# The first nine projection blocks on raw x, with the norm factor put on the results

## The reference

```python
def rmsnorm(x, g):
    x32 = x.astype(jnp.float32)
    r = lax.rsqrt(jnp.mean(x32 * x32, axis=-1, keepdims=True) + EPS)
    return (x32 * r * g.astype(jnp.float32)).astype(x.dtype)

def project_in(x, pos, g_attn_norm, w_in, ...):
    xn = rmsnorm(x, g_attn_norm)
    z = jnp.einsum('bsd,de->bse', xn, w_in)
    qa, ka, va, oa, ia, fa, cq, ckv, kr, gate_a, gate_b = split_cols(z)
    ...
```

## Time and profile before

| | us |
|---|---|
| median of the runs shown (three, 2769.88 to 2774.63) | 2773.61 |
| the profiled execution | 2768.64 |
| its span | 2766.5 |
| TensorE busy | 2729.1 |
| VectorE busy | 1638.6 |
| ScalarE busy | 1281.1 |
| GpSimd busy | 411.4 |

### The profile page before, as it was taken

The page is one execution under the profiler, slowest core; times in us unless marked ns, Lnnn a source line. Parts: engine busy times, 40 slices in busy tenths (PEclk is TensorE's granted clock), DMA queues, the critical chain, the costliest instruction groups (busy, mean ns, idle before and its releaser), DMA issues.

```text
span 2766.5 us, 54080 instructions
## 1 busy us (share of the span) xinstructions
PE 2729.1 (99%) x19156; PEld 2603.4 (94%) x19156; DVE 1638.6 (59%) x2739; ACT 1281.1 (46%) x2286; POOL 411.4 (15%) x770
## 2 busy tenths in 40 slices
PE   9998899999999999999999999999999999999999
PEld 9865799999999989999999999999999999999999
DVE  5466866666566654555454444466767644667754
ACT  5536665565556544444443333344444433444432
POOL 0102343443334310000000000022000000000010
PEclk9999999999999999999999999999999999999999
DMA  7524121221122177656657566576555456555575
GB/s 241 199 70 111 35 51 51 66 57 53 50 63 64 38 236 208 191 172 187 189 172 203 166 174 169 166 189 173 166 167 166 138 166 185 168 167 159 146 188 132
DMA packets 737356, 393.55 MB, mean 142 GB/s; under 512 B 109262, under 2 KB 719288, under 8 KB 736560
## 3 DMA queue, kind: packets, MB, share of 16 engines
q1 hardware_dynamic: 709132, 378.61, 47.7%
q10 hardware_dynamic: 27508, 11.54, 1.5%
q0 software_dynamic: 512, 0.83, 0.3%
HBM read 370.49 MB, written 22.75 MB: 142 GB/s over the span
## 4 chain that ended last, share of the span: by engine, by line
PE 60%; DVE 1%; issue 1%; ACT 1%; ACTq 0%; DVEq 0%
PE bank L302 19%; PE bank L307 19%; PE bank L303 19%; PE bank L2748 0%; ACT sqm L2812 0%; PE bank L2726 0%; PE bank L2736 0%; DVE hn L2913 0%; PE bank L2733 0%; PE bank L2722 0%; DVE hn L2908 0%; ACT dws L2806 0%; DVE ns L2895 0%; PE bank L2721 0%; PE bank L2710 0%
## 5 line engine op out<-in xcount | busy, mean ns | idle before, releaser
L290 DVE TENSOR_TENSOR w_lo_b<-stage,w_hi_b 128x2048 fp32r<-128x2048 f32 (+2 forms) x286 | 612.4, 2142 | 404.6 <-ACT w_hi_b L283 400.1
L283 ACT ACTIVATE w_hi_b<-stage 128x2048 fp32r<-128x2048 f32 (+1 forms) x284 | 508.3, 1790 | 559.4 <-PE bank L307 496.0
L302 PE MATMUL bank<-xnH,w_hi_b 128*128 128x288 f32 (+1 forms) x2736 | 741.0, 299 | 2.6 <-PEq L191 2.6
L303 PE MATMUL bank<-xnL,w_hi_b 128*128 128x288 f32 (+1 forms) x2736 | 735.6, 295 | 0.0
L302 PEld LDWEIGHTS bank<-xnH,w_hi_b 128*128 128x128 f32 (+1 forms) x2736 | 514.0, 188 | 12.1 <-issue 11.5
L303 PEld LDWEIGHTS bank<-xnL,w_hi_b 128*128 128x128 f32 (+1 forms) x2736 | 513.6, 188 | 0.3
L1741 PE MATMUL bank<-uk_all,lat 128*128 128x384 f32 (+1 forms) x1344 | 441.7, 329 | 14.1 <-DVE lat L2535 6.0
L1743 PE MATMUL bank<-uk_all,lat 128*128 128x384 f32 (+1 forms) x1344 | 435.6, 324 | 0.0
L307 PE MATMUL bank<-xnH,w_lo_b 128*128 128x288 f32 (+1 forms) x2736 | 390.8, 295 | 0.0
L307 PEld LDWEIGHTS bank<-xnH,w_lo_b 128*128 128x128 f32 (+1 forms) x2736 | 372.1, 188 | 0.0
L1741 PEld LDWEIGHTS bank<-uk_all,lat 128*128 128x128 f32 x1344 | 253.9, 189 | 28.8 <-issue 20.0
(11 more groups left out here) (537 smaller groups left out, 3749.5 us busy)
## 6 DMA issues: line engine op xcount, KB each, us to landing
stage<-in_w_in_dram SPq DMA_DIRECT2D x88, 1024.0 KB, 5.4
stage<-in_w_up_dram SPq DMA_DIRECT2D x88, 1024.0 KB, 5.4
stage<-in_w_down_dram SPq DMA_DIRECT2D x64, 704.0 KB, 4.6
raw<-in_cache_kv_latent_dram SPq DMA_DIRECT2D x256, 64.0 KB, 1.8
stage<-in_w_branch_a_dram SPq DMA_DIRECT2D x16, 1024.0 KB, 5.5
stage<-in_w_branch_b_dram SPq DMA_DIRECT2D x16, 1024.0 KB, 5.6
stage<-in_w_out_dram SPq DMA_DIRECT2D x16, 1024.0 KB, 5.8
vals<-in_cache_kv_latent_dram SPq DMA_DIRECT2D x60, 256.0 KB, 2.9
```

Of the source, the lines that this page charges most:

```text
L283: act.activation(h, a, ACT.Copy).then_inc(w_hi, 1)
L290: dve.tensor_tensor(lo, a, h.bitcast(F32), ALU.subtract).then_inc(w_lo, 1)
L302: pe.matmul(out, hi, xH(k), start=first and k == 0, stop=False)
L303: pe.matmul(out, hi, xL(k), start=False, stop=False)
```

## The change

The first nine blocks are computed on x with the gain but without the row factor. x is turned by plain transposes against the identity as soon as it lands, so norm_t isn't needed for it, and the clearing of unused rows goes. The squares, the root and the factor are made later, after the high parts of blocks 0 and 2 on ScalarE and after the low parts of blocks 0 to 2 on VectorE; TensorE spreads the factor over all partitions by a product of ones with norm_t, after the low products of block 2, and VectorE keeps it as rx. VectorE now takes each result out of its bank with a multiplication by rx (`scaled_out`), ScalarE squares the copy (`square`). Normalised x for the later phases is made beside it: GpSimd adds xnH and xnL of each chunk in the loop (`summed`), VectorE multiplies four chunks at a time by rx (`normed_sum`), ScalarE rounds them (`normed_high`), VectorE takes the rest (`normed_low`), SP writes them out in four parts each between chunks of the query weights. On TensorE block 1 runs twelve chunks behind, block 2 after the low products of block 0, and in each of the first twelve steps of the loop a product of constants with 64 columns stands in block 1's place. Warm products are nine instead of eighteen. On SP the gain rows go first and weight block 0 is loaded in two halves between the halves of x.

```diff
@@ sync
+                    x_half(0)
+                    sp.dma_start(x_tok[0:N_S, 2, :], A["x_sample"].rearrange("b s d -> (b s) d")).then_inc(x_in2, 16)
+                    first_weights(0, w_first)
+                    x_half(1)
+                    first_weights(1, w_landed[0])
...
-                    sp.wait_ge(x_L, KC)
-                    sp.dma_start(xnL_dram, xnL[:].bitcast(F32)).then_inc(xL_out, 16)
-                    chunk(6)
-                    sp.wait_ge(x_H, KC)
-                    sp.dma_start(xnH_dram, xnH[:].bitcast(F32)).then_inc(xH_out, 16)
+                    def normed(g):
+                        part = slice(g * XG, (g + 1) * XG)
+                        sp.wait_ge(x_nL, g + 1)
+                        sp.dma_start(xnL_dram[:, part, :], xr[:, part, :]).then_inc(xL_out, 16)
+                        sp.wait_ge(x_nH, g + 1)
+                        sp.dma_start(xnH_dram[:, part, :], xrH[:, part, :].bitcast(F32)).then_inc(xH_out, 16)
+                    for i in range(4):
                         chunk(i)
+                        normed(i)
@@ tensor
-                    warm(16)
-                    pe.wait_ge(rows_in, 16 * 9)
-                    pe.transpose(bank[3][:, 0:60], rows[:], ident[0:60, 0:60]).then_inc(vec_t, 1)
-                    warm(2)
+                    warm(9)
...
-                            tr = pe.matmul(bank[4 + c % 4][:, t0:t0 + n], x_tok[:, t, chunk_], norm_t[:, t, 0:n], start=True, stop=True)
+                            if c % (KC // 2) == 0:
+                                pe.wait_ge(x_in[t][c // (KC // 2)] if t < 2 else x_in2, 16)
+                            tr = pe.transpose(bank[4 + c % 4][:, t0:t0 + n], x_tok[0:n, t, chunk_], ident[0:n, 0:n])
...
+                    LAG = 12
...
+                    for k in range(KC):
+                        pe.wait_ge(x_L, k + 1)
+                        if k + 4 < KC:
+                            turn_x(k + 4)
+                        high_half(0, k)
+                        if k >= LAG:
+                            high_half(1, k - LAG)
+                        else:
+                            pe.matmul(bank[2][:, 0:64], ident, cst[:, 0:64], start=True, stop=True)
+                    for k in range(KC - LAG, KC):
+                        mm = high_half(1, k)
+                    mm.then_inc(x_hb, 1)
+                    low_half(0)
+                    for k in range(KC):
+                        high_half(2, k)
+                    low_half(1)
+                    low_half(2)
+                    pe.wait_ge(x_dg, 3)
+                    pe.matmul(bank[4][:, 0:T], ones, rw[:, 0:T], start=True, stop=True).then_inc(x_rb, 1)
@@ scalar
-                        if c in (0, 2, 4, 6):
-                            quarter_high(0, c // 2)
-                        if c in (8, 10, 12, 14):
-                            quarter_high(2, c // 2 - 4)
+                        if c in (1, 4, 8, 11):
+                            quarter_high(0, (1, 4, 8, 11).index(c))
+                    for g in range(4):
+                        quarter_high(2, g)
+                    norms()
...
+                    def normed_high(g):
+                        part = slice(g * XG, (g + 1) * XG)
+                        act.wait_ge(x_nr, g + 1)
+                        act.activation(xrH[:, part, :], xr[:, part, :], ACT.Copy).then_inc(x_nH, 1)
...
+                        square(n - 2)
+                        if n > 4:
+                            normed_high(n - 5)
...
+                    act.wait_ge(xL_out, 16 * 4)
+                    act.wait_ge(xH_out, 16 * 4)
@@ gpsimd
+                    def summed(c):
+                        pool.wait_ge(x_L, c + 1)
+                        pool.tensor_tensor(xr[:, c, :], xnH[:, c, :].bitcast(F32), xnL[:, c, :].bitcast(F32), ALU.add).then_inc(x_sum, 1)
...
+                    for c in range(KC):
+                        summed(c)
+                        if c in (9, 11, 13):
+                            second_high((c - 9) // 2)
+                    second_high(3)
@@ vector
+                    def scaled_out(m):
+                        dve.wait_ge(w_done, m + 1)
+                        if m == 8:
+                            dve.tensor_tensor(zkr[:], bank[0][0:W0, 0:T], rx[0:W0], ALU.mult).then_inc(z_free[0], 1)
+                            return
+                        dve.tensor_tensor((cqT if m < 4 else ckvT)[:, m % 4, :], bank[m % 4][:, 0:T], rx[:], ALU.mult).then_inc(z_free[m % 4], 1)
+
+                    def normed_sum(g):
+                        part = slice(g * XG, (g + 1) * XG)
+                        dve.wait_ge(x_sum, (g + 1) * XG)
+                        dve.tensor_tensor(xr[:, part, :], xr[:, part, :], rx[:].unsqueeze(1).broadcast_to([P, XG, T]), ALU.mult).then_inc(x_nr, 1)
+
+                    def normed_low(g):
+                        part = slice(g * XG, (g + 1) * XG)
+                        dve.wait_ge(x_nH, g + 1)
+                        dve.tensor_tensor(xr[:, part, :].bitcast(F32R), xr[:, part, :], xrH[:, part, :].bitcast(F32), ALU.subtract).then_inc(x_nL, 1)
...
+                        if n == 3:
+                            dve.wait_ge(x_rb, 1)
+                            dve.tensor_copy(rx[:], bank[4][:, 0:T]).then_inc(x_rx, 1)
+                            dve.wait_ge(x_rx, 1)
+                            scaled_out(0)
+                            scaled_out(1)
+                        else:
+                            scaled_out(n - 2)
+                        if 4 <= n < 8:
+                            normed_sum(n - 4)
+                        if n > 4:
+                            normed_low(n - 5)
```

## The result

The changed kernel took 2780.78 us (median of eight runs, 2776.40 to 2782.57), the kernel before 2769.98 beside it (eight runs, 2768.15 to 2774.63). The ratio is 1.0035, with a 95% interval of 1.0027 to 1.0044: slower by 10.8 us, where 2771.2 was forecast and 2777.0 was the end of the range. The forecast took its 2.4 us off a median of three runs, 2773.61; the eight runs put the kernel before 3.6 us lower. So the miss is 9.6 us in the time and 13.2 in the difference. The profiled execution took 2780.72 us, its span is 2778.9.

What follows compares the result with a forecast made beforehand. TensorE, busy 2729.1 of 2766.5 us, was taken as the bound. An earlier first product and cheaper turning, less constant products and GpSimd's hold, gave 2.4 us off the 2773.6 median: 2771.2, range 2767.0 to 2777.0.

Steps and rivals of the forecast that it cites:

- rival C: Head: TensorE's passes fall back to double length after standing still; 2774.0 (first stretch) or 2778.0 (both), chance 0.12 and 0.08.
- from an idle time between those two: TensorE's clock: passes stayed fast after 1.89 us idle, slow after 6.0; the fall decides somewhere between.
- First product: Head: TensorE's first weight product starts near 13.0, 3.6 us early, with x_sample landed at 9.3.
- The allowance of 0.5 for gains and copy: Ahead of the loop: 0.5 us allowed for the gains' transpose and copy, after four chunks turned at 10.9.
- Turning a chunk: Head and loop: three plain transposes per chunk cost 0.32 us, against 0.69 before.
- Step of the loop: Loop: transposes, two products and a 64-column product of constants take 0.83 us a step (0.69 to 0.86).
- GpSimd's adds: Loop: each 128x288 add of xnH and xnL takes 0.77 us pace (0.63 to 0.85), 0.81 long.
- The hold: Loop's end: GpSimd stands still 2.2 us beside VectorE's low half of block 0; TensorE waits 1.9 us.
- From the low products of block 0 to block 3: After the loop: low halves 0 to 2, block 2's high part and ones times the factor, 11.0 us.
- The factor's cover: Before block 3: factor ready by 38, TensorE asks at 40.8; cover 2.8 us, costed at nothing.
- Blocks 3 to 8: TensorE's period 6.4 us, no waits inside; cover of 0.8 before the queries, up to 1 us if gone.
- What the head gains or loses should arrive at the end: Whole kernel: TensorE has almost no idle time after the head, so changes there carry to the end.
- The gain of 2.4: Head: block 3 starts at 41.3 against 43.75, so the kernel gains 2.4 us.

Runs made afterwards that it cites:

- e10_pause_timed: Changed kernel with 12 warm products instead of 9 and four more behind the gains' transpose, eleven runs: 2770.49 us, ratio 0.9996 to the kernel before.
- e1_pause: Changed kernel with 12 warm products instead of 9 and four more behind the gains' transpose, single run: 2767.44 us, kernel before 2771.24 beside it.
- e8_best: As e7_order, without products of constants in the loop, three warm products behind the gains' transpose, casts after chunks 4, 6, 8, 11: 2765.29 us, ratio 0.998 to before.
- e9_pause_nofill: Changed kernel without products of constants in the loop, TensorE's waits ahead of the loop left as they were: 2776.88 us.
- e7_order: Changed kernel with x_sample and first x_prompt halves ahead of gains, waits filled, block 1 six chunks behind, six 256-column constant products, earlier casts: 2771.07 us.
- e2_fill256: Changed kernel with 256 instead of 64 columns in the loop's twelve products of constants, waits ahead of the loop left: 2772.8 us.

## Why the prediction was wrong

The step that failed is the price of rival C. The mechanism stood there, with its place, and had 0.2. Its slow stretch was taken "as long as the first, 5.6 us" and priced at 2.8. It lasted 23.9. Block 3 starts 9.7 us later than in e10_pause_timed, where the clock stays (10.1 counted from the first product); that is the term, and it was mis-sized by a factor of 3.5. With the 0.8 us by which the queries of e10_pause_timed start later than those of the kernel before, it makes the 10.5 us at the queries. The reason: the length was taken from a stretch of 256-column products of constants, and the way back depends on what runs. Twelve steps of transposes and two products didn't bring the clock back; 256-column products did in 3.4 us. Nor does it decide "from an idle time between those two", 1.89 and 6.0 us: the waits here were 1.02 and 1.54 us. Of the twelve traces the five in which TensorE waited longest for x_sample amid the turning (0.48, 0.71, 1.02, 1.19 and 1.33 us) fell to 0.50 before 16; in the other seven it waited 0.41 once and else not at all, and the clock stayed. The second wait, for xnL, was absent in two of the five. That is an association in a few executions and no rule. How the fall is set off stays open. e1_pause and e10_pause_timed are one kernel and differ in it; how soon the warm passes are through decides how long TensorE waits for x_sample, and that varies from execution to execution.

Point by point, with the clock taken out by e10_pause_timed (block 3 at 43.99, forecast 41.3):

- First product: 13.0 forecast, 15.43 measured. Wrong by 2.4, and most of it is x_sample, which landed at 11.2 instead of 9.3. Behind x it took 7.6 us from issue to landing; in e8_best, issued at 1.15 ahead of x_prompt, it took 3.7. The halves of x ahead of it were late already: in e9_pause_nofill TensorE gets the second half tile at 9.69, where 8.5 was forecast. The allowance of 0.5 for gains and copy was right (13.08 to 13.60).
- Turning a chunk: 0.32 forecast from the earlier trace rows, 0.49 in the loop and 0.56 for the first four. Pass behind it: 0.24 to the next, where 0.13 was taken. The loop of before had shown it (16.64 to 16.86). Products of constants: 0.17, where 0.24 was taken.
- Step of the loop: 0.83 forecast, range to 0.86; 1.02 at the upper level, 1.77 at the lower. Twelve steps: 10.0, 11.8 and 20.1.
- GpSimd's adds: 0.77 pace and 0.81 length forecast; 0.75 pace in a row of six, 0.79 long. Right.
- The hold: one add near 3 us beside the low half of block 0 was forecast, 2.78 was measured, over VectorE's 2.28. The mechanism was right. By the Trainium skill ("SBUF — State Buffer", Who interferes with whom) the two shut each other out, and the trace agrees. But the 1.9 us of TensorE's waiting didn't come, because TensorE was later by then (in e10_pause_timed it takes up the last quarter at 32.05, 0.2 us after GpSimd's cast): 5.4 us from step 12 to the low products of block 0 in e10_pause_timed, 7.3 forecast. Two errors that nearly cancel, 1.8 late and 1.9 early.
- From the low products of block 0 to block 3: 11.0 forecast, 10.9 measured.
- The factor's cover: right. Squares from 39.76, root at 46.29, block 3's high part done at 48.4, all before 53.66, with no wait of TensorE.
- Blocks 3 to 8: no wait inside them, as forecast. They and the step to the queries take 40.87 instead of 40.30, 0.26 of it a wait for VectorE's first query weights: the cover of 0.8 was gone, at a cost of 0.3, within "up to 1 us".

```profile
94.53 0.37 PE L803 MATMUL bank<-cqH,w_hi_b 128*128 128x288 f32 x1 [0.26 <-DVE w_lo_b L1374]
```

- "What the head gains or loses should arrive at the end": right, 10.5 at the queries and 10.8 in the medians. On the way it isn't constant. In the changed kernel the end of the attention falls into the lower level for longer than in before, and its next phase starts 14.2 us late (294.18 against 280.01); by 1018 it is 11.3. Whether that belongs to the change or to this execution, one trace can't tell. The changed kernel, then the kernel before:

```profile
280.00:284.00 4.00, 1.93 (x7) 0.75 0.00 0
284.00:300.00 16.00, 10.04 (x37) 0.50 0.18 55
...
284.00:300.00 16.00, 16.00 (x75) 0.86 0.21 49
```

- The gain of 2.4 was wrong too. With the clock kept, block 3 starts 0.2 us later than before and the queries 0.8 later, and the ratio is 0.9996 (0.9987 to 1.0005): no difference that can be measured. The missing part is x_sample and the step of the loop, less the wait for GpSimd that didn't come.

## What to carry to other kernels

Where a change takes padding work off TensorE ahead of a loop, weigh not only the idle time that might make the clock fall but what runs behind it: the slow stretch may be over in 3.4 us or last as long as that loop. Fill the wait ahead of the loop with products (8 passes, 2.0 us, in a wait of 1.5) rather than sprinkle small ones inside it: with them the clock stayed in e10_pause_timed, and in e1_pause it fell and was back before the loop. And see that what gates the first product is issued first: x_sample behind two gain rows and two halves of x landed 1.9 us later than forecast. With it in front the first product came 2.0 us earlier in e7_order and 3.0 in e8_best, where fewer warm products stood ahead of it too.

## What the runs showed of the hardware

- Which level a loop runs at can depend on the level at which it starts. The same loop of three transposes, two products of 288 columns and 64 columns of constants per chunk runs at 1.00 for all its length when it starts there (e10_pause_timed), and at 0.50 for nearly all its length when the clock falls at its start (the changed kernel, 15.7 to 35.5, then 4.1 us of back-to-back products until it rose). TensorE is shown as 100% busy in both.
- The way back took 3.4 us with 256-column products in the loop (e2_fill256), 1.4 and 4.1 us of back-to-back products of 288 columns behind the light loop (e9_pause_nofill, the changed kernel).
- Executions of one kernel can differ: in e1_pause the clock was lost for 3.4 us, in e10_pause_timed never. By the Trainium skill ("TensorE: Matmul & The Clock Gate", Part 1) the number of slow products at a start varies from run to run of one kernel; this pair agrees: the same 24 passes took 7.38 and 8.40 us. The granted clock reads 1.00 at that start, at either pace.
- A GpSimd add of 0.79 us beside a VectorE instruction with two SBUF inputs of 2.28 takes 2.78. Four in a row beside three such take 9.27, and the three take 8.6 instead of 6.8 (e8_best).
